# Spreading routing gates by four tokens per step, with double-banked transposed rows, four row buffers, and the high and low gate rows made on ScalarE

## The reference

```python
s = einsum('nhpc,hpkc->nhpk', q, keys32)            # 8 heads, 2 halves, 128 keys each
top_s, top_i = lax.top_k(s, 16)                     # 16 best keys of each half
best_s, best_c = lax.top_k(cand_s, 16)              # 16 best of the 256 sums
expert_idx = take_along_axis(cand_i, best_c)        # key_a * 128 + key_b
gate = softmax(best_s)
act = gelu(einsum('nhkd,nd->nhk', expert_u[expert_idx], x_blk))
out = einsum('nhk,nhkd->nd', gate * act, expert_v[expert_idx])
```

## Time and profile before

| what | value |
|---|---|
| median of 3 runs | 1870.82 us (1869.05 to 1873.73) |
| the profiled execution, its own time | 1864.57 us |
| its span, first to last instruction | 1862.8 us |
| PE busy | 1731.7 us, 93% |
| DVE busy | 1325.5 us, 71% |
| ACT busy | 664.8 us, 36% |
| POOL busy | 799.4 us, 43% |
| DMA traffic | 413.80 MB, mean 222 GB/s |

### The profile page before, as it was taken

One profiled execution on the slowest core, in us unless ns is written; L12 is line 12 of the kernel. 1 busy time (PEld: TensorE's weight loads), 2 busy tenths in 40 slices (PEclk: granted clock), 3 DMA queues, 4 the chain that ended last, 5 costly groups with the idle time before them and its releaser, 6 DMA issues.

```text
span 1862.8 us, 24594 instructions
## 1 busy us (share of the span) xinstructions
PE 1731.7 (93%) x9066; PEld 1536.5 (82%) x9066; DVE 1325.5 (71%) x1866; ACT 664.8 (36%) x801; POOL 799.4 (43%) x454
## 2 busy tenths in 40 slices
PE   6999999989968999799979999786899999999997
PEld 5777788868868999799979999776788888888886
DVE  2555511125887999989998998865888777778777
ACT  5444432252223444344434434321333333322232
POOL 3333244324314344743476876664533333333331
PEclk9999999989989999999999999998999999999999
DMA  5222123322226455565547878898899999999992
GB/s 157 70 68 67 57 84 91 98 67 79 79 87 221 151 203 197 205 226 191 207 154 248 316 274 285 298 385 331 302 391 378 355 358 359 350 353 349 350 344 102
DMA packets 211428, 413.80 MB, mean 222 GB/s; under 512 B 11408, under 2 KB 150704, under 8 KB 205744
## 3 DMA queue, kind: packets, MB, share of 16 engines
q1 hardware_dynamic: 154352, 228.63, 36.2%
q0 software_dynamic: 36864, 134.23, 19.9%
q10 hardware_dynamic: 20160, 50.34, 7.1%
HBM read 360.73 MB, written 52.43 MB: 222 GB/s over the span
## 4 chain that ended last, share of the span: by engine, by line
PE 44%; DVE 15%; DMA 7%; ACT 2%; POOL 2%; issue 1%; SPq 1%; ACTq 0%; DVEq 0%; POOLq 0%
PE psum L1111 25%; PE psum L1052 15%; PE psum L1043 3%; DVE ul L1312 3%; DMA expert_gate<-grid 3%; DVE ring L1387 3%; DMA u_raw<-in_expert_u 2%; PE psum L1075 1%; DVE hot L1373 1%; DVE hot L1377 1%; DVE hot L1375 1%; DVE eq L1322 1%; DMA ring<-in_expert_u,index 1%; DMA v_raw<-in_expert_v 1%; POOL ring L1258 1%
## 5 line engine op out<-in xcount | busy, mean ns | idle before, releaser
L1052 PE MATMUL psum<-xTh,uh 128*128 128x384 f32 x1024 | 359.3, 351 | 2.0 <-DVE ul L1312 2.0
L1052 PE MATMUL psum<-xTl,uh 128*128 128x384 f32 x1024 | 347.6, 339 | 0.0
L1052 PE MATMUL psum<-xTh,ul 128*128 128x384 f32 x1024 | 347.3, 339 | 0.0
L1258 POOL DMA_INDIRECT ring<-in_expert_v,index x128 | 177.9, 1390 | 337.3 <-DVE acc L1392 300.2
L218 POOL TENSOR_TENSOR wl<-raw,wh 128x1024 fp32r<-128x1024 f32 x72 | 172.4, 2402 | 328.0 <-ACT wh L490 328.0
L1111 PE MATMUL psum<-vh,dwh 128*128 128x512 f32 x768 | 298.9, 389 | 1.6 <-DVE dwl L1400 1.6
L1111 PE MATMUL psum<-vl,dwh 128*128 128x512 f32 x768 | 298.8, 389 | 0.0
L1111 PE MATMUL psum<-vh,dwl 128*128 128x512 f32 x768 | 298.8, 389 | 0.0
L1188 ACT ACTIVATE vh<-v_raw 128x4096 fp32r<-128x4096 f32 x32 | 116.2, 3632 | 340.9 <-PE psum L1111 293.5
L1258 POOL DMA_INDIRECT ring<-in_expert_u,index x128 | 179.6, 1403 | 90.2 <-DVE ring L1387 65.7
L1312 DVE TENSOR_TENSOR ul<-psum,uh 128x1024 fp32r<-128x1024 f32 x128 | 156.1, 1219 | 83.8 <-ACT uh L1139 83.7
(11 more groups left out here) (192 smaller groups left out, 2915.0 us busy)
## 6 DMA issues: line engine op xcount, KB each, us to landing
u_raw<-in_expert_u SPq DMA_DIRECT2D x128, 512.0 KB
v_raw<-in_expert_v SPq DMA_DIRECT2D x32, 2048.0 KB, 12.1
expert_act<-hb ACTq DMA_DIRECT2D x128, 192.0 KB, 2.6
expert_gate<-grid ACTq DMA_DIRECT2D x12, 2048.0 KB, 9.2
dh<-expert_act SPq DMA_DIRECT2D x32, 768.0 KB, 4.4
dg<-expert_gate SPq DMA_DIRECT2D x32, 768.0 KB, 6.6
raw<-in_w_in SPq DMA_DIRECT2D x40, 512.0 KB, 3.8
raw<-in_w_q SPq DMA_DIRECT2D x16, 512.0 KB, 4.0
```

What stands on the lines that cost most here:

```text
L1052: last = nc.tensor.matmul(zb[s][:, 0:DT], w[s][:, c, :], x[:, c, 0:DT], start=(c == 0 and n == 0), stop=(c == C - 1 and n == 2))
L1258: nc.gpsimd.indirect_dma_start(out=ring[k][:], out_offset=None, in_=tables[x // SLOTS], in_offset=bass.IndirectOffsetOnAxis(ap=index[:, x ...
```

## The change

Four things change together.

1. **Banks.** `utp` becomes two pairs of banks (0, 1 and 6, 7), used in turn. The transposes of a step then wait for DVE's `low` of two steps back, not of the step just before. `gp` shrinks from four banks to two (2, 3).
2. **Spread by 4 tokens.** `spread` runs in each of two successive steps with 4 matmuls, where it ran once in two steps with 8. `evac` is one copy of 1024 columns, in each of those steps, and `gather` adds 4 tokens at a time. They come one to two steps later than before after the batch's one-hot rows are made.
3. **High and low gate rows on ACT.** DVE makes only the two one-hot rows (`one_hots`); ACT scales the second by the gate's high and then its low part with 16 copies of 128 columns, each with a per-partition scale (`hi`). DVE's multiply and POOL's are gone. `send` moves ahead of `gelu` in its step.
4. **Buffers and table.** `raw` has four buffers in place of two, so that SP loads up to three steps ahead; all its loads are issued before SP waits for the gate table (`g_out`), where six loads stood behind that wait. EVERY goes from 34 to 36, and PACE spreads the 128 sparse rows more evenly: from 6 to 18 in the ranking steps, and from 51 + 41 to 71 over the last stretch.

```diff
-FIRST, EVERY = 12, 34
+FIRST, EVERY = 12, 36
-EVAC = {hot_step(k) + 1: k for k in range(BATCHES)}
-GATHER = {hot_step(k) + 3: k for k in range(BATCHES)}
+SPREAD = {hot_step(k) + 2 + h: 2 * k + h for k in range(BATCHES) for h in range(2)}
+GATHER = {hot_step(k) + 3 + h: 2 * k + h for k in range(BATCHES) for h in range(2)}
-PACE = ((8, 12, 4), (12, 36, 6), (36, 46, 10), (46, 70, 6), (70, 80, 10), (80, 114, 51), (114, 128, 41))
+PACE = ((8, 14, 6), (14, 38, 18), (38, 50, 15), (50, 74, 18), (74, 128, 71))
-    utp = psum[:, 0:2 * T]
+    utp = psum[:, 0:2 * T], psum[:, 6 * T:8 * T]
-    gp = [psum[:, i * T:(i + 1) * T] for i in (6, 7, 2, 3)]
+    gp = psum[:, 2 * T:4 * T]
...
-            def transposes(s, r):
-                pe.wait_ge(u_in[s], r * 16 + 16)
-                pe.wait_ge(ut_lo[1 - s], r + s)
+            def transposes(n, q=0):
+                s = n % 2
+                pe.wait_ge(u_in[n % 4], q * 16 + (n // 4 * 16 + 16))
+                pe.wait_ge(ut_lo[s], q * 2 + n // 2)
...
+            def hi(k):
+                s = k % 2
+                act.wait_ge(S["hot_eq"], k + 1)
+                for n in range(8):
+                    t = 8 * k + n
+                    last = nc.scalar.activation(hot[s][:, n, 1, :], hot[s][:, n, 2, :].bitcast(F), ACT.Copy,
+                                                scale=gate_hi[:, t:t + 1].bitcast(F))
+                last.then_inc(hot_hi[s], 1)
+                act.wait_ge(hot_hi[s], k // 2 + 1)
+                for n in range(8):
+                    t = 8 * k + n
+                    last = nc.scalar.activation(hot[s][:, n, 2, :], hot[s][:, n, 2, :].bitcast(F), ACT.Copy,
+                                                scale=gate_lo[:, t:t + 1])
+                last.then_inc(hot_lo[s], 1)
...
                 if n + 1 < STEPS:
                     high(n + 1)
+                if n in SEND:
+                    send(SEND[n])
+                if n in HOT:
+                    hi(HOT[n])
                 gelu(n)
...
-                if n in EVAC:
-                    evac(EVAC[n])
+                if n in SPREAD:
+                    evac(SPREAD[n])
...
-            def hot_lo(k):
-                s = k % 2
-                pool.wait_ge(hot_ready[s], k // 2 + 1)
-                low_ = hot[s][:, :, 2, :]
-                nc.gpsimd.tensor_tensor(low_, low_.bitcast(F), gate_lo[:, 8 * k:8 * k + 8].unsqueeze(2).broadcast_to([P, 8, KEYS]),
-                                        ALU.mult).then_inc(hot_key[s], 1)
...
-                dve.wait_ge(S["hot_eq"], k + 1)
-                nc.vector.tensor_tensor(hi, low_.bitcast(F), gate_hi[:, cols].bitcast(F).unsqueeze(2).broadcast_to([P, 8, KEYS]),
-                                        ALU.mult).then_inc(hot_ready[s], 1)
...
-        u_raw = [m.put(f"u_raw{i}", 100 + 4 * i, [P, D]) for i in range(2)]
+        u_raw = [m.put(f"u_raw{i}", kb, [P, D]) for i, kb in enumerate((100, 104, 136, 140))]
```

More of the change, by code:

```diff
@@ L919, in experts_program @@
     grid = m.put("grid", 112, [P, KEYS, 32])
-    parts = [m.put(f"parts{i}", 128 + 8 * i, [P, 8, 2, KEYS]) for i in range(2)]
+    parts = [m.put(f"parts{i}", 128 + 4 * i, [P, 4, 2, KEYS]) for i in range(2)]
     hot = [m.put(f"hot{i}", 144 + 12 * i, [P, 8, 3, KEYS], R) for i in range(2)]
@@ L1052, in products, with step @@
                         last = nc.tensor.matmul(zb[s][:, 0:DT], w[s][:, c, :], x[:, c, 0:DT],
-                                                start=(c == 0 and n == 0), stop=(c == C - 1 and n == 2))
+                                                start=(c == 0 and i == 0), stop=(c == C - 1 and i == 2))
                 last.then_inc(u_mm[s], 1)
[L1056 to L1059, removed]
+            def step(n, q=0):
+                transposes(n + 1, q)
+                products(n, q)
@@ L1079, in _, with spread @@
[L1079 to L1082, removed]
-            last.then_inc(ut_full[0], 1)
-            with pe.Fori(0, FIRST // 2) as r:
-                for s in range(2):
-                    step(s, r)
+            def spread(x, q=0):
+                s, half = x // 2 % 2, x % 2
+                if half == 0:
+                    pe.wait_ge(hot_ready[s], q + (x // 4 + 1))
+                    pe.wait_ge(hot_hi[s], q + (x // 4 + 1))
+                    pe.wait_ge(hot_lo[s], q + (x // 4 + 1))
+                pe.wait_ge(S["g_evac"], q * 4 + (x + PRIMED))
+                for n in range(4):
+                    at = 4 * half + n
+                    last = nc.tensor.matmul(gp[:, n * 2 * P:(n + 1) * 2 * P], hot[s][:, at, 0, :],
+                                            hot[s][:, at, 1:3, :].rearrange("p g k -> p (g k)"), start=True, stop=True)
+                last.then_inc(g_full[s], 1)
@@ L1097, in _ @@
-            with pe.Fori((FIRST + EVERY * DB) // 2, HALF - 1) as r:
-                for s in range(2):
-                    step(s, r)
-            step(0, HALF - 1)
-            step(1, HALF - 1, ahead=False)
+                for n in range(n0 + 1, n0 + 4):
+                    step(n)
+                with pe.Fori(0, 8) as q:
+                    for n in range(4):
+                        step(n0 + 4 + n, q)
+                        spread(32 * b + n, q)
+            for n in range(FIRST + EVERY * DB, STEPS - 1):
+                step(n)
@@ L1108, in down @@
                     b, half = k // 2, k % 2
+                    if first and k >= 4:
+                        pe.wait_ge(h_done[k - 4], HALF + PRIMED)
                     for j in range(G4):
```

121 lines of the change are left out of this document (53 added, 68 removed).

## The result

The changed kernel takes 1825.97 us (median of 4 runs, 1822.15 to 1828.26), against 1872.28 us for the kernel before in the runs beside it (median of 4). The ratio is 0.975, with a 95% interval of 0.9725 to 0.9776. The forecast was 1820 us in a range of 1790 to 1852, faster with a chance of 0.89.

A forecast was written before the change was run, and what follows sets the result against it. PE, busy 93%, was taken as near enough to a bound that only its open stretches pay. Stage excess falls from 109 to 58 us (11 + 8 + 23 + 5 + 5 + 6): 1870.8 - 51 = 1820 us, range 1790 to 1852.

The forecast's parts named there:

- The excess of the stage: 128 steps, 806 us long against 697 us needed: 109 us of excess, of which 58 us would stay.
- first 12 steps: Start of the stage: 15 us of excess, second banks give back 4 in four late steps, 11 us stay.
- finding of keys, twice: Steps behind the ranking steps, finding of keys and 1.25 rows a step close together: 4 us left twice, 8 in all.
- the two exps: Exps of later blocks, with two table loads, fall on a loaded ACT: 2.5 us each, 5 in all.
- gate steps of the last group (sends): Sends wait ahead of copies for POOL's last addition; outside ranking pairs about 1 us each shows, 5 in all.
- end of the stage: DVE's long subtraction ahead of its last `low`, and its new wait for the last transposes: 6 us.
- The price of a copy: ACT's 128-column copies with a scale: 0.29 us each, 4.8 us for 16 with the wait; bounds 3.4 and 6.2 us.
- The rival in which copies don't overlap: Copies on ACT take 0.385 us each, ACT bounds everywhere: 64 us more, 1884 us; chance 0.07.
- The loop in the ranking steps: ACT's copies wait for DVE's one-hot: 12.0 us a pair against PE's 11.04, 23 us over 24 ranking pairs.
- ACT nearly full: Gate groups: ACT's work 10.9 us a pair against PE's 11.04, 98% occupied; without ranking PE sets the pace.
- The rival by which the end is not relieved: From 1000 us DMA itself is the bound, late steps stay slow: gain about 5 us, 1866 us; chance 0.06.
- The 15.3 us wait and POOL's waits: Last stretch: PE's wait for `u_raw`, waits for POOL and late `low`s expected to go, with nothing left for them.

The follow-up runs named there:

- the last run: Changed kernel with one-hots first, send between high and low copies, and 2 instead of 8 sparse rows in the six key-finding steps: 1800.2 us, ratio 0.9622.

## Why the prediction was right

Its range and its main mechanism held, one term was well off, and that its time came so near is in part luck. Point by point:

- **The excess of the stage.** 109 us before, 58 forecast. Measured by the same rule, the stage runs from its first transposes at 525.2 us to 1290.6 us, 765 us, against 695 us that the steps need (the 692 us of the prediction and 3 for the first transposes): 70 us. The profiled executions differ by 1864.57 - 1824.93 = 39.6 us, where 51 were forecast, so the forecast for the profiled execution, 1813.6 us, was 11 us off. The medians differ by 46 us, because the profiled execution of the kernel before lay 8 us below its median and that of the changed kernel only 1 us: about half of the closeness of 1820 to 1826 us is luck.
- **Term by term**, from the starts of PE's transposes in the profiled execution:

| excess in us | forecast | measured |
|---|---|---|
| first 12 steps | 11 | 8 |
| 24 ranking pairs | 23 | 25 |
| finding of keys, twice | 8 | 20 |
| the two exps | 5 | 5 |
| gate steps of the last group (sends) | 5 | 7 |
| end of the stage | 6 | 5 |

- **The price of a copy.** Eight copies took 2.45 us, and one alone 0.39, so the starts lie (2.45 - 0.39) / 7 = 0.29 us apart: the middle value taken. ACT's busy time, 884.3 us, was forecast as near 880. The rival in which copies don't overlap was to decide from about 0.365 us (its own terms, 51 + 3.6 us over 768 copies on top of 0.29, give 0.36) and was out.
- **The loop in the ranking steps.** 12.0 us forecast, 12.07 measured. That it is a loop over two engines and not the load of either is shown by two runs: taking 12.7 us of work off DVE in the stretch changed nothing, and reordering DVE's work without removing any gained 12.5 us. The 23 us are what the ranking pairs take beyond PE's pace, and not what undoing the loop gives back.
- **ACT nearly full.** 10.9 us in a pair against PE's 11.04 was forecast; in the pair shown above ACT is occupied for 10.6. It has a consequence that I did not draw: the second banks, which I counted only for the first 12 steps with 4 us, are worth 18 us, 5 of them in those steps and some 13 behind them.
- **The end of the stage.** The waits for expert rows went, as forecast. Both causes named are shown, each by undoing it: the row table, 31 us, and the loads behind the wait for the gate table, 15.5 us. The rival by which the end is not relieved was priced as a gain of 5 us from the two DVE-bound stretches less the loop; the steps from 12 to 88 show no such gain but a loss of 11 us. Up to step 88 the changed kernel is nearly 7 us behind; without relief at the end nothing would have been gained.
- **The step that was off in size** is "behind the ranking steps ... I leave 4 us twice, 8 in all". Two steps in the first of these stretches took 22.1 us in place of 11.06, and two in the second 20.1, so 11 and 9 us, 20 in all. PE's transposes in the first:

```profile
767.55 1.03 PE L1042 MATMUL psum<-ident,u_raw 128*128 128x128 f32 x8
...
780.12 1.52 PE L1042 MATMUL psum<-ident,u_raw 128*128 128x128 f32 x8
...
789.67 1.04 PE L1042 MATMUL psum<-ident,u_raw 128*128 128x128 f32 x8
```

The rows that I read for it had shown the mechanism, and I had counted the POOL product that goes, not the key products that stay. That is 12 us more than forecast, all by which the excess of the stage was undersized; the other terms were off by up to 3 us each and cancel in their sum. How much of the 20 us is DVE beside POOL's key products and how much ACT's wait of 7.8 us for the addition queued behind them stays open.
- **The 15.3 us wait and POOL's waits** were forecast to go without anything in their place at the end. PE's waits for `low` there are down to 4.6 us from 1220 us on, so that held.

The parts do not add up: undone they cost 31 (the table), 25 (the copies, with the place of the send), 18 (the banks) and 15.5 us (the order of the loads), 90 us together, against a gain of 46. A reading that fits, but that only the table's run alone tests, is that each removes an obstacle behind which the others' gain would be lost; the table alone even loses 12 us. No run tells what the four row buffers alone or the spread by four tokens alone are worth, and that stays open.

## What to carry to other kernels

When work is moved to an idle engine, sum the new chain from one step to the next across all engines that it passes, and not only the load of each: here ACT and DVE each had time to spare, and the 12.07 us loop through both still set the pace. Such a loop is undone by moving work that nothing waits for out from between its links; here that gave 12 us, and not the whole of what the pairs lost. And undo the parts of a compound change one at a time before keeping or dropping any: a table worth 31 us in company cost 12 us alone.

## What the runs showed of the hardware that was not expected

- Beside POOL's products of two SBUF tensors (5.87 us for two of 1024 columns), DVE operations with two SBUF inputs stretched from 1.2 to 3.4 us, while `low`, with one input in PSUM, took 1.20 to 1.23 us in all 128 steps. In the last run one of them lay beside a key product:

```profile
767.35 1.21 DVE L1318 TENSOR_TENSOR ul<-psum,uh 128x1024 fp32r<-128x1024 f32 x1
...
767.57 2.39 POOL L1285 TENSOR_TENSOR eq<-eq,pick_f 128x1024 f32<-128x1024 f32 x1 [1.23 <-DVE eq L1328]
```

In the trace of before, one such DVE operation took 3.42 us beside 2.53 us of POOL. That their sum and not their overlap is what counts is read from these traces; no run here measured it by itself.
- The granted clock was 1.00 from 606 to 742 us after, where PE waited 6.0 us in nine waits of at most 1.3 us. In the finding of keys (742 to 812) it was 0.95: right behind waits of 2.7 and 3.8 us it was 0.55 in the mean of 780 to 785 us and 0.76 in that of 785 to 790 us, hence partly at its lower level of 1.2 GHz, and 1.00 in the rest.
